# First layer of a two-block model: output gate by exponential and logarithm, head norms one slot earlier, weight splits in slots of their own, constants awaited where they are used

## The reference

```python
def even_mixer(x, w_in, b_in, ml_norm, w_out):
    u = x @ w_in + b_in
    mq, mk, mv, mo, mi, mf, fq, fk, fv, ff = split_sizes(u, [...])
    h_ml = mlstm_chunkwise(heads(mq, 4), heads(mk, 4), heads(mv, 4), mi..., mf...)
    h_ml = head_norm(h_ml, ml_norm)...                      # over the 128 channels of each of 4 heads
    h_ml = (jax.nn.sigmoid(mo.astype(jnp.float32)) * h_ml)  # the output gate
    h_fx = forgetting_attention(heads(fq, 8), heads(fk, 8), heads(fv, 8), ff...)
    return jnp.concatenate([h_ml, h_fx], axis=-1) @ w_out
```

## Time and profile before

| | us |
|---|---|
| median of 3 runs | 2368.05 (2365.91 to 2369.34) |
| the profiled execution | 2362.74 |
| its span | 2360.9 |
| TensorE busy | 2228.8 |
| VectorE, ScalarE, GpSimd busy | 1334.9, 910.9, 148.7 |
| mean granted TensorE clock | 0.977 |

### The profile page before, as it was taken

One profiled execution on the slowest core, in us unless ns is written; L12 is line 12 of the kernel. 1 busy time (PEld: TensorE's weight loads), 2 busy tenths in 40 slices (PEclk: granted clock), 3 DMA queues, 4 the chain that ended last, 5 costly groups with the idle time before them and its releaser, 6 DMA issues.

```text
span 2360.9 us, 26680 instructions
## 1 busy us (share of the span) xinstructions
PE 2228.8 (94%) x10624; PEld 1813.8 (77%) x10632; DVE 1334.9 (57%) x2025; ACT 910.9 (39%) x1514; POOL 148.7 (6%) x148
## 2 busy tenths in 40 slices
PE   8998899999998979999998799999999989999998
PEld 6766688888877748888886687777787877888887
DVE  6355656556347764655634527855677655555634
ACT  3134444334334354433432434344444534333421
POOL 1000013000006001300000000000001420000000
PEclk9999899999999999999999999999999999999999
DMA  5211123323313202333332222202222002333332
GB/s 185 91 52 64 44 73 106 97 94 113 98 63 98 81 27 72 104 95 97 116 98 63 72 81 72 80 28 72 81 72 72 1 1 81 98 98 98 107 102 77
DMA packets 50811, 190.34 MB, mean 81 GB/s; under 512 B 5632, under 2 KB 5632, under 8 KB 49920
## 3 DMA queue, kind: packets, MB, share of 16 engines
q1 hardware_dynamic: 50688, 188.63, 24.9%
HBM read 186.51 MB, written 2.10 MB: 80 GB/s over the span
## 4 chain that ended last, share of the span: by engine, by line
PE 56%; DVE 4%; ACT 1%; issue 1%; DMA 1%; another core or an unknown queue 0%; ACTq 0%; DVEq 0%
PE bank L346 16%; PE bank L348 16%; PE bank L347 16%; PE bank L772 3%; PE bank L531 1%; DVE small L1437 1%; PE bank L446 1%; PE bank L745 1%; PE bank L509 1%; DMA ring<-stream 1%; DVE arena L1464 0%; PE bank L520 0%; PE bank L893 0%; PE bank L486 0%; PE bank L494 0%
## 5 line engine op out<-in xcount | busy, mean ns | idle before, releaser
L346 PE MATMUL bank<-xs,whi 128*128 128x512 f32 (+1 forms) x1952 | 769.2, 394 | 23.9 <-DVE wlo L1411 11.3
L348 PE MATMUL bank<-xs,wlo 128*128 128x512 f32 (+1 forms) x1952 | 750.4, 384 | 0.0
L347 PE MATMUL bank<-xs,whi 128*128 128x512 f32 (+1 forms) x1952 | 749.8, 384 | 0.0
L1411 DVE TENSOR_TENSOR wlo<-ring,whi 128x1024 fp32r<-128x1024 f32 x334 | 419.3, 1260 | 323.6 <-ACT whi L924 323.2
L924 ACT ACTIVATE whi<-ring 128x1024 fp32r<-128x1024 f32 x334 | 350.0, 1053 | 293.7 <-DMA ring<-stream 293.5
L346 PEld LDWEIGHTS bank<-xs,whi 128*128 128x128 f32 x1952 | 369.4, 189 | 109.7 <-issue 21.5
L347 PEld LDWEIGHTS bank<-xs,whi 128*128 128x128 f32 x1952 | 369.4, 189 | 71.1 <-issue 3.8
L348 PEld LDWEIGHTS bank<-xs,wlo 128*128 128x128 f32 x1952 | 368.7, 189 | 71.6
L346 PE MATMUL bank<-whi,xs 128*128 128x512 f32 (+1 forms) x816 | 321.2, 394 | 19.2 <-ACT xs L936 8.8
L347 PE MATMUL bank<-wlo,xs 128*128 128x512 f32 (+1 forms) x816 | 318.3, 390 | 0.0
L348 PE MATMUL bank<-whi,xs 128*128 128x512 f32 (+1 forms) x816 | 318.2, 390 | 0.0
(11 more groups left out here) (298 smaller groups left out, 1930.5 us busy)
## 6 DMA issues: line engine op xcount, KB each, us to landing
ring<-stream SPq DMA_DIRECT2D x334, 512.0 KB, 3.6
arena<-gains SPq DMA_DIRECT2D x5, 1024.0 KB, 5.5
arena<-xt SPq DMA_DIRECT2D x4, 512.0 KB, 5.9
arena<-xn SPq DMA_DIRECT2D x1, 2048.0 KB, 7.9
out<-arena SPq DMA_DIRECT2D x4, 512.0 KB, 2.6
con<-consts SPq DMA_DIRECT2D x1, 744.0 KB, 10.5
arena<-brow SPq DMA_DIRECT2D x1, 512.0 KB, 11.3
par<-params SPq DMA_DIRECT2D x1, 407.5 KB, 8.4
```

What stands on the lines that cost most here:

```text
L346: nc.tensor.matmul(out, ah, bh, start=first, stop=False)
L347: nc.tensor.matmul(out, ah, bl, start=False, stop=False)
L348: return nc.tensor.matmul(out, al, bh, start=False, stop=last)
L1411: V.tensor_tensor(wlo[:, v % SLOTS, :], ring[:, v % SLOTS, :], whi[:, v % SLOTS, :], ALU.subtract).then_inc(wlo_done, 1)
```

## The change

1. **Loads.** par goes ahead of unit 1 and has its own semaphore; then units 1 to 3, con, brow, units 4 and 5, and pw last with its own semaphore, which TensorE awaits before the pooling products of the second layer.
2. **Constants.** TensorE runs mq and mk before it waits for con, brow and the setups. ScalarE waits only for par before small0; VectorE starts the gate logits with no wait for constants, and makes its three casts after it has read mq.
3. **Head norms.** `floor` at 4h+4, the mean of squares at 4h+7, logarithm and exponential at 4h+8, final product at 4h+9. `den` and the square stay.
4. **Gate.** VectorE's reciprocal goes; sigmoid(x) = exp(-ln(1 + exp(-x))). 1 is added at the slot of the first exponential (with a cap at 1e38), the logarithm and the second exponential come one slot later on ScalarE, the multiplication one slot after that. All of mo is three slots earlier (pieces of unit j in slots 2+7j to 7+7j, exponential at 8+7j).
5. **Splits.** The calls in even slots go. Units 27 to 33 are split in slots 3, 8, 13, 17, 20, 24, 27 of the attention, one in each; `fk`'s fourth evacuation no longer splits.
6. **Mixed operand.** Its rows are split in slots 30 to 33 (high) and one slot later (low), row 7 after the last slot. In slots 32, 33 and 34 TensorE multiplies units 0, 1, 2 of out0 for token tile 1; the first two units' order of tiles is then 1 (done), 2, 0, and 3.

```diff
-            sp.dma_start(ring[:, 1, :], stream[1]).then_inc(ring_sem[1], 16)
-            sp.dma_start(par[:], params).then_inc(in_sem, 16)
-            sp.dma_start(ring[:, 2, :], stream[2]).then_inc(ring_sem[2], 16)
+            sp.dma_start(par[:], params).then_inc(par_sem, 16)
+            for s in (1, 2, 3):
+                sp.dma_start(ring[:, s, :], stream[s]).then_inc(ring_sem[s], 16)
             sp.dma_start(con[:], consts).then_inc(in_sem, 16)
-            sp.dma_start(pw[:], poolw).then_inc(in_sem, 16)
             sp.dma_start(arena[:, 20:22, :], brow...).then_inc(in_sem, 16)
-            for s in range(3, SLOTS):
+            for s in range(4, SLOTS):
                 sp.dma_start(ring[:, s, :], stream[s]).then_inc(ring_sem[s], 16)
+            sp.dma_start(pw[:], poolw).then_inc(pw_sem, 16)
...
-        MO_FIRST, MO_STEP = 5, 7
+        MO_FIRST, MO_STEP = 2, 7
+        fox_splits = {3: FIRST["mo"] + 2, 8: FIRST["mo"] + 3, 13: FIRST["out0"], 17: FIRST["out0"] + 1, 20: FIRST["out0"] + 2, 24: FIRST["out0"] + 3, 27: FIRST["out0"] + 4}
+        operand_at = {30: (0, 1), 31: (2,), 32: (4, 5), 33: (3, 6)}
...
# TensorE
+                if n >= 32:
+                    for half in (0, 1):
+                        out0_part(n - 32, 1, half)
...
             run_units("small0", SCALAR, "x")
+            run_units("mq", VECTOR)
+            run_units("mk", SCALAR)
             pe.wait_ge(in_sem, 16 * nloads)
             pe.wait_ge(gpsimd_out, gpsimd_at.find("setup"))
             pe.wait_ge(vector_out, vector_at.find("setup"))
-            run_units("mq", VECTOR)
-            run_units("mk", SCALAR)
...
-            out_products(0, "ln1_0")
+            token_products("out0", out0_part, "ln1_0", tiles=((1, 2, 0), (3,)))
...
# ScalarE, beside_fox
-                    unit_done("mo", j)
+                    act.wait_ge(units_done, FIRST["mo"] + j + 1)
                     A(gate[:, j, :], bank[7][:], ACT.Exp, bias=small[:, 32 + j:33 + j], scale=-1.0)...
-                elif n % 2 == 0:
-                    split_units(FIRST["mo"] + max(0, (n - MO_FIRST) // MO_STEP) + AHEAD)
+                if n - 1 in mo_evacuate:
+                    act.wait_ge(vector_out, vector_at.find("mo", "one", j))
+                    A(gate[:, j, :], gate[:, j, :], ACT.Ln)...
+                    A(gate[:, j, :], gate[:, j, :], ACT.Exp, scale=-1.0)...
+                if n in fox_splits:
+                    split_units(fox_splits[n])
+                for k in operand_at.get(n, ()):
+                    mixed_high(k)
...
# VectorE, beside_fox
-                if n % 2 == 0:
-                    split_units(FIRST["mo"] + max(0, (n - MO_FIRST) // MO_STEP) + AHEAD)
-                if n - 1 in mo_evacuate:
-                    V.tensor_scalar(gate[:, j, :], gate[:, j, :], 1.0, None, ALU.add)...
-                    V.reciprocal(gate[:, j, :], gate[:, j, :])...
+                if n in fox_splits:
+                    split_units(fox_splits[n])
+                for k in operand_at.get(n - 1, ()):
+                    mixed_low(k)
+                if n in mo_evacuate:
+                    V.tensor_scalar(gate[:, j, :], gate[:, j, :], 1.0, 1e38, ALU.add, ALU.min)...
+                if n - 2 in mo_evacuate:
                     V.tensor_tensor(MIX[:, j, :], MIX[:, j, :], gate[:, j, :], ALU.mult)...
...
-            split_operand("mix0", MIX)
+            mixed_low(7)
```

More of the change, by code:

```diff
@@ L395, in piece, with token_parts @@
                     reader[b] = (VECTOR if name == "fq" else SCALAR, ("read", name, j))
-            def token_products(name, slot, ready, nxt, head=2, tiles=((2, 3, 0), (1,))):
-                n, u0, tail = COUNT[name], FIRST[name], COUNT[name] - TAIL
-                waited, claimed = set(), set()
+            def token_parts(name, slot, ready):
+                n, u0 = COUNT[name], FIRST[name]
+                waited, claimed, done = set(), set(), {}
                 def part(j, tt, half):
+                    if (j, tt, half) in done:
+                        return done[j, tt, half]
                     if j not in waited:
@@ L412, in part, with token_products @@
                         claim(b)
-                    return products(bank[b][:], (xhi[:, slot(j), t], xlo[:, slot(j), t]), (whi[:, s, w], wlo[:, s, w]), j == 0, j == n - 1)
+                    done[j, tt, half] = products(bank[b][:], (xhi[:, slot(j), t], xlo[:, slot(j), t]), (whi[:, s, w], wlo[:, s, w]), j == 0, j == n - 1)
+                    return done[j, tt, half]
+                return part
+            def token_products(name, part, nxt, head=2, tiles=((2, 3, 0), (1,))):
+                n, tail = COUNT[name], COUNT[name] - TAIL
                 for j in range(head):
@@ L595, in head_norms @@
                     reader[7] = (VECTOR, ("hn", "var", h))
+            out0_part = token_parts("out0", lambda k: k, lambda k, tt: pe.wait_ge(vector_out, vector_at.find("xl", "mix0", k)))
             def beside_fox(n):
@@ L698, in values_and_pool @@
                     claim(6 + j % 2)
+                    pe.wait_ge(pw_sem, 16)
                     pe.wait_ge(vector_out, vector_at.find("pooled", j))
@@ L908, in _ @@
                 tensor_at.mark("stage", "mix2")
-                token_products("out2", lambda k: k, lambda k, tt: pe.wait_ge(vector_out, vector_at.find("xl", "mix2", tt)), "rms2", head=4, tiles=((0, 1, 2), (3,)))
+                token_products("out2", token_parts("out2", lambda k: k, lambda k, tt: pe.wait_ge(vector_out, vector_at.find("xl", "mix2", tt))), "rms2", head=4, tiles=((0, 1, 2), (3,)))
                 tensor_at.mark("stage", "rms2")
@@ L1133, in _ @@
             attention("fox", fox_steps, beside_fox)
[L1134 to L1137, removed]
+            mixed_high(7)
             root_ready()
@@ L1552, in query_unit @@
                 name, j = ml_evacuate.get(n, (None, 0))
-                if name == "fk":
+                if name == "fk" and n < ML_SLOTS:
                     split_units(FIRST["fk"] + j + AHEAD)
@@ L1579, in head_norms, with mixed_low @@
                     V.tensor_tensor(scale[h % 2], bank[7][:], floor[h % 2], ALU.add).then_inc(vector_out, vector_at.next("hn", "var", h))
+            def mixed_low(k):
+                dve.wait_ge(scalar_out, scalar_at.find("xh", "mix0", k))
+                V.tensor_tensor(xlo[:, k, :], MIX[:, k, :], xhi[:, k, :], ALU.subtract).then_inc(vector_out, vector_at.next("xl", "mix0", k))
             def beside_fox(n):
@@ L1584, in beside_fox @@
                 query_unit(ML_SLOTS + n)
-                if n % 2 == 0:
-                    split_units(FIRST["mo"] + max(0, (n - MO_FIRST) // MO_STEP) + AHEAD)
-                if n - 1 in mo_evacuate:
-                    j = mo_evacuate[n - 1]
+                if n in fox_splits:
[3 more added lines that the diff above has]
+                if n in mo_evacuate:
+                    j = mo_evacuate[n]
                     dve.wait_ge(scalar_out, scalar_at.find("read", "mo", j))
[L1590 to L1593, removed]
+                    V.tensor_scalar(gate[:, j, :], gate[:, j, :], 1.0, 1e38, ALU.add, ALU.min).then_inc(vector_out, vector_at.next("mo", "one", j))
+                if n - 2 in mo_evacuate:
+                    j = mo_evacuate[n - 2]
+                    dve.wait_ge(scalar_out, scalar_at.find("mo", "gate", j))
                     V.tensor_tensor(MIX[:, j, :], MIX[:, j, :], gate[:, j, :], ALU.mult).then_inc(vector_out, vector_at.next("gated0", j))
@@ L1668, in _ @@
             split_units(1)
[L1670 to L1674, removed]
+            split_units(FIRST["mq"] + 1)
+            absolute("gate0", ("read", "small0", 0))
             split_units(FIRST["mq"] + 2)
-            absolute("gate0", ("read", "small0", 0))
             dve.wait_ge(scalar_out, scalar_at.find("gate0", "ln"))
@@ L1694, in _ @@
                 V.tensor_scalar(mq[:, j, :], bank_of("mq", j)[:], col("b_mq", j), P ** -0.5, ALU.add, ALU.mult).then_inc(vector_out, vector_at.next("read", "mq", j))
+            dve.wait_ge(in_sem, 16 * nloads)
+            V.tensor_copy(idb[:], ident).then_inc(vector_out, vector_at.next())
+            V.tensor_copy(mtb[:], con[:, K_MT:K_MT + P]).then_inc(vector_out, vector_at.next())
+            V.tensor_copy(mqb[:], con[:, K_MQ:K_MQ + P]).then_inc(vector_out, vector_at.next("setup"))
             clear_parts(0)
```

40 lines of the change are left out of this document (25 added, 15 removed).

## The result

| | before | changed |
|---|---|---|
| median of 4 runs each, us | 2367.69 (2365.91 to 2369.34) | 2339.77 (2337.33 to 2340.91) |
| profiled execution, its span | 2362.74, 2360.9 | 2337.33, 2335.5 |
| ratio | | 0.9881, 95% interval 0.9864 to 0.9898 |

The account below looks back on a forecast made before the run. TensorE, busy 94%, was taken as the bound, so only its waits and half-rate clock could be won. Start 4.5, mLSTM 3.1, attention 16.0 and end 5.0 sum to 28.6 us: 2334 profiled, 2339.4 median, range 2330 to 2353.

Parts of the forecast that it names:

- Start: Kernel start: TensorE's 2.8 us wait for the constants' casts and 1.7 of lower clock go, gaining 4.5 us.
- Head norms: mLSTM slots 10 and 14: TensorE's waits for the head's bank go, gaining 3.1 us.
- Gate: Attention gates: without VectorE's four 3.35 us reciprocals, TensorE's waits of 3.7, 1.2 and 0.75, and 4.4 behind them go.
- Waits left by the splits: Seven attention slots holding a weight split: TensorE still waits 1.4, 1.2, 1.0 and 0.4 in four, together 4.0 us.
- First slots: First attention slots: of the 4.2 us of TensorE waits there, 1.1 remains.
- End: Attention's end: out0's 4.6 us wait and 2.6 of half rate go, 2.2 of waits appear in slot 32; 5.0 gained.
- No drop between 180 and 290: Attention, 180 to 290 us: left-over waits of 1.4 us and less keep TensorE's clock at 1.00; a drop refutes this.
- rival (c): Attention and mLSTM: left-over waits each lower the clock, in five places at 2.2 us, so 11 us: 2350; chance 0.12.
- (a): Attention: slack is larger than reckoned, the 7.3 us of left-over waits vanish, 35.9 us gained: 2332; chance 0.13.
- (b): Start: gain not won, as unit 1 or 2 is late behind more bytes: 2344; chance 0.05.
- (d): Attention: in-order queues pay more for eleven new slots than the reciprocal cost, 50.6 us: about 2383, slower; chance 0.04.
- (e): Whole change: waits only change their names, ScalarE late instead of VectorE, time within 0.2%: 2366; chance 0.03.

Follow-up runs that it names:

- e1: Changed kernel with the start as before (old load order, waits for all constants, casts before mq): median 2343.78 us, ratio to before 0.9894.
- e2: Changed kernel with the four head-norm steps back in their old slots: median 2349.45 us, ratio to before 0.9914.
- e5: Changed kernel with the weight splits called as before (even slots, ahead of each gate, at fk's fourth evacuation): median 2346.80 us, ratio to before 0.9901.
- e3: Changed kernel with VectorE's reciprocal back in the gate, without ScalarE's logarithm and second exponential: median 2353.86 us, ratio to before 0.9927.
- e6: Kernel before with only the gate's formula changed, from reciprocal to logarithm and exponential: median 2353.75 us, ratio to before 0.9924.
- e4: Changed kernel with all operand rows split after the last slot and no out0 matmuls beside the attention: median 2340.07 us, ratio to before 0.9871.
- e9: Changed kernel with the attention's end as before and mo's pieces and gates three slots later, as before: median 2342.82 us, ratio to before 0.9885.
- e7: Changed kernel with the mixed operand's rows split earlier, spread over slots 25 to 33: median 2339.08 us, ratio to before 0.9875.

## Why the prediction was right

**The total.** The forecast of the median, 2339.4, met 2339.77, and part of that is luck. The sum of 28.6 us was 3.2 too large in the traces: 2334 was forecast for the profiled execution, which took 2337.33. The 5.3 us between profiled execution and median, carried over from the kernel before, were 2.4 in the changed one, and that made up for it.

**Start, 4.5 us.** The traces say 3.95, where the changed kernel's first half rate ended 1.5 us later than before's (0.7 us lost), and 4.8 with medians 5.0 apart on one chip (e1). Right, cover and all: nothing waited for the casts or for unit 1.

**Head norms, 3.1 us.** Right for the bank: 2.9 us were won between mk and the attention's first logits. e2 measures 4.6 there, with 1.7 of half rate that the kernel before did not have, and 4.8 more in the attention's first slots, where I had put the gain down to the product of head 2 and the two splits together. The splits of that slot are 2.4 us, nearly all given back by logits 12 (e5); the norms' share is larger.

**Gate.** I counted 3.7 + 1.9 + 4.4 of waits and 3.7 of half rate for the first three reciprocals, 13.7 us. e3 says 11.3 by logits 25 and e6 11.1 by logits 31. Right in mechanism, and some 2.5 us too large. The fourth reciprocal I held to be part of the 4.6 before out0; it was, but taking it out alone left 4.14 (e6), since the split and the multiplication took its place.

**Waits left by the splits, 4.0 us.** Measured 2.5 (the two L530 lines, 3.0, less the 0.46 of slot 32). My worst slots, 10, 19 and 26, came out at 0.4, 0.3 and 0.3 instead of 1.4, 1.2 and 1.0; slots 22 and 29, which I had at nothing, have 0.4 and 0.6. The walk along the queue was right in kind. From the end of slot 8's transposes (197.00) to the scaled weights it took 4.7 us where I reckoned 5.1, and TensorE worked 4.5 us in that time where I reckoned 3.6: it has 14 value matmuls there, and I had counted seven.

**First slots, 1.1 left.** 1.17 + 0.27 = 1.4 us. Right.

**End, 5.0 us.** The sum is about right for what changed at the end, and the cause is wrong. Laying out0's matmuls and the operand's rows beside the last slots is worth nothing in the stretch (e4: -0.5). It removes a wait of 2.0 and makes one of 0.19 into 1.23, with 1.7 us of half rate behind it; the wait of 0.46 is there with it and without it. What took the old wait from 4.6 to e4's 2.0 is, as the queues of before, e6 and e4 show, that neither the last gate nor a split stands right ahead of the operand any more.

**Clock.** "No drop between 180 and 290" failed once, at 258.64, behind a wait of 1.23: 3.42 / 2 = 1.7 us. That, and a first half-rate stretch that ended at 12.88 instead of 11.4 us (0.7), is most of the difference between 28.6 and the 25.4 of the spans. Of rival (c) one place in five came true. The gain cannot be added up from the single undoings: with the start and the times to the norm they are 4.8 + 9.3 + 11.1 + 4.8 - 0.5 = 29.5 us, and e9 adds 5.9, more than the 25.4 there are. Part of this is the clock: e2 and e3 have 10.2 and 6.8 us more at half rate than the changed kernel. The rest was not taken apart.

The attention's last value products end at 265.4 us (264 forecast). Rivals (a) and (b) did not come: 6.3 us of the 7.3 of left-over waits are there, and no wait stands before mq or mk. Rivals (d) and (e) are refuted: no logarithm slot is followed by a wait above 1.3 us, and the waits went instead of changing names.

## What to carry to other kernels

On an in-order engine beside a busy TensorE, look for the one long instruction first: put back, a 3.35 us reciprocal cost 2.4 to 3.7 us of waiting each time, with half rate behind three of four, and the two operations of 0.63 on a half-idle engine that replace it left no wait in the slots behind the second and third gate. A producer in the very slot in which its result is wanted is worth moving by one slot, even where its own work is small. Before laying work beside the last slots of a pipeline, check which single queue it lands on: here it cost as much as it saved, and moving it to other slots of the same queues won nothing but a missing half rate.

## What the runs showed of the hardware

The same wait does not always lower TensorE's clock. The 2.5 us in mLSTM slot 10 left it at 1.00 before; in e6, with the same wait in the same slot, it is at half rate:

```profile
152.30:155.70 3.40, 3.40 (x6) 0.50 0.00 0
```

Waits of 1.23 behind 0.46 were followed by half rate in the changed kernel and its repetition, and not in e1, with the same waits in the same slots. Before the norm's first transpose, waits of 2.19 (e7) and 2.05 (e5) left the clock at 1.00, and waits of 1.86 (before) and 2.04 (e1) were followed by half rate. So a wait's length alone does not say what follows it.

So whole stages differ between executions of one kernel with no edit in them. The same 872 recorded matmuls, between the same two transposes in the second layer, first in the changed kernel's profile and then in its repetition's:

```profile
666.46:885.90 219.44, 189.87 (x872) 0.95 0.20 65
```

```profile
665.98:888.83 222.85, 192.99 (x872) 0.94 0.20 64
```

They take 3.4 us more in the second, which has 27.3 us at half rate there instead of 20.5. A gain of 2 to 3 us in one stage is therefore seen in that stage's trace and not in a median of five runs.
